# Gathering each page of selected keys and values with four indirect DMAs of 2 KB rows in place of one of 8 KB rows

## The chip, the cores and the metric

The kernel runs on one core of one Trainium2 chip. The metric is the time of one execution on the device, in microseconds, as the median of several runs. The core has TensorE (PE: matrix products, with weight loads shown as PEld), VectorE (DVE), ScalarE (ACT), GpSimd (POOL) and SyncE (SP); DMAs are issued from the queues of SP, ACT and POOL and run on 16 DMA engines that all queues share.

## What is computed

One decoder layer for a prompt of 512 tokens and for 8 samples of 8 new tokens each. A sample has 2048 past tokens in paged pools (16 pages of 128 tokens; a token has 2 heads of 64 floats, 512 bytes). Of the layer, what matters here is the sample's attention over selected blocks:

```python
def gather_past(pool, page_table, new_rows):
    b = page_table.shape[0]
    old = pool[page_table].reshape(b, -1, N_KV_HEADS, HEAD_DIM)
    return jnp.concatenate([old, new_rows], axis=1)
...
ksb = to_blocks(gather_past(cache_k_slc[l], page_table, ks))
vsb = to_blocks(gather_past(cache_v_slc[l], page_table, vs))
...
s = jnp.einsum('bkgqd,bkqmd->bkgqm', qh, k_sel).astype(jnp.float32) * scale
p_slc = masked_softmax(s, (pos_sel <= q_pos[:, None])[:, :, None])
o_slc = jnp.einsum('bkgqm,bkqmd->bkgqd', p_slc.astype(v_sel.dtype), v_sel)
```

The kernel computes the scores against all 2048 past keys of a sample and masks the blocks that are not selected, so it reads every key and value once: 1 MB of keys and 1 MB of values a sample. Beside this there are a compressed branch (from other pools), a window branch (512 tokens from a state), a gated convolution, projections and a feed-forward net.

## The kernel before

All of the program is written by hand, one instruction stream per engine, with semaphores between them. Order in a stream is the order of the code.

Stages, by the profile's time: up to about 125 us the compressed caches of the samples are gathered and compressed; up to about 280 us the input projections and the convolution run; from about 280 to 372 us the samples' attention runs, in four pairs of samples (`gp` 0 to 3), together with products for the adaLN rows (`ada_step`); then the prompt's attention, the output projection and the feed-forward net, which last to the end.

**The ring of pages.** `cring` has `CR` = 4 slots of 2048 columns, 8 KB per partition, 1 MB in all. Loads into it are numbered: 0 to 15 are the compressed caches, and from 16 on, four per pair: pages 16 + 4 gp + b are the selected keys of sample 2 gp + b, pages 18 + 4 gp + b its values (b is 0 or 1). "Page" here is the content of one slot: all 2048 tokens of one sample. Partition p holds 16 consecutive tokens, 8 KB that lie together in the pool. The row numbers for the gather come from `idx`, written once by VectorE (line 1540) from the page table; for the compressed caches from `idq` (line 1537), where a page is already gathered by four indirect DMAs of 2 KB per partition (line 891).

**GpSimd's stream** (from line 905): `key_pages(0)`, `value_pages(0)`, `key_pages(1)`, then for gp = 1, 2: `key_pages(gp + 1)`, `value_pages(gp)`, and at last `value_pages(3)`. `key_pages` waits for the transposes that free its two slots (`keys_turned`), issues two gathers and then the two window loads of 256 KB (`window`, line 883, rows of 2 KB). `value_pages` waits for the last value product of the pair before (bank `("O", gp - 1, 0)`), issues two gathers and two window loads. Behind these come the store of the adaLN rows (line 946) and the scaling of the prompt's probabilities (line 954).

**VectorE's stream.** A page of keys is transposed whole (`turn_page`, line 1829), the window's keys in `turn_window` (line 1838). For gp = 0 the order is: masked scores (line 1910), `turn_window(0)`, compressed scores (1786), window scores, `cmp_probs(1)`, `turn_page(1, 0)`, `turn_page(1, 1)`, `cmp_groups(1)` (lines 1796 and 1797), `turn_window(1)`, then the ranking of blocks (1803 to 1817). For later pairs `turn_page(gp + 1, 0)` stands ahead of the window scores.

**TensorE's stream** (from line 2841): for each pair `values(gp - 1)` (lines 2771 and 2774: x = 0 from the pages of values, x = 1 from the window), compressed and window scores, transposes of probabilities (2439), two `ada_step` (2474), importance and compressed values (2640, 2646), then `scores(gp + 1)` (line 2714), which waits for both page transposes of its pair. `values` waits for the two pages of values.

**SyncE** loads the adaLN weights for the next `ada_step` (line 718, 512 KB each) as their ring is freed.

Of the kernel before, what the change touches and what calls it, by code (L numbers as in the profile page):

```python
# [22 lines left out]
U32 = mybir.dt.uint32  # L23

D = 1024
SEQ, NB, NQ = 512, 8, 8
# [18 lines left out]
CR = 4  # L45
# [8 lines left out]
C_ID, C_P8, C_ROPE, C_ROPEC, C_CAUS, C_CMB, C_CM01, C_NEW, C_WIN, C_OVL, C_TRI, C_ONE, C_END = np.cumsum(  # L54
    [0, 128, 8, 80, 16, 512, 124, 124, 256, 512, 32, 900, 128]).tolist()
# [51 lines left out]
def constants():  # L107

    c = np.zeros((128, C_END), np.float32)
    p = np.arange(128)  # L110
    c[:, C_ID:C_ID + 128] = np.eye(128)
    inv = np.float32(500000.0) ** (-np.arange(8, dtype=np.float32) * np.float32(2.0) / np.float32(16))

    def cs(pos):
        ang = pos.astype(np.float32)[:, None] * inv[None, :]
        return np.concatenate([np.cos(ang), np.sin(ang)], 1)

    for t in range(5):
        c[:, C_ROPE + 16 * t:C_ROPE + 16 * t + 16] = cs(t * 128 + p if t < 4 else PAST + p % NQ)
    c[:, C_ROPEC:C_ROPEC + 16] = cs(p * 16 + 31)  # L120
    c[:, C_CAUS + 384:C_CAUS + 512] = np.where(p[None, :] <= p[:, None], 0, NEG)
    n = np.arange(PNC)
    for t in range(4):
        ok = n[None, :] * 16 + 31 <= (t * 128 + p)[:, None]
        c[:, C_CMB + PNC * t:C_CMB + PNC * (t + 1)] = np.where(ok, 0, NEG)
        c[:, C_CM01 + PNC * t:C_CM01 + PNC * (t + 1)] = ok
    b2, q = p // 64, p % 8
    k = np.arange(TS)
    for gp in range(4):
        ok = (k[None, :] // 8 == (2 * gp + b2)[:, None]) & (k[None, :] % 8 <= q[:, None])  # L130
        c[:, C_NEW + 64 * gp:C_NEW + 64 * gp + 64] = np.where(ok, 0, NEG)
    i = np.arange(512)
    c[:, C_WIN:C_WIN + 512] = np.where((4 * (i % 128) + i // 128)[None, :] > q[:, None], 0, NEG)
    j = np.arange(32)
    c[:, C_OVL:C_OVL + 32] = (p[:, None] * 16 < (j[None, :] + 1) * 64) & (p[:, None] * 16 + 32 > j[None, :] * 64)
    t30 = np.arange(NC1)
    c[:, C_TRI:C_TRI + 900] = np.where(t30[None, :] < t30[:, None], -TIE, 0).reshape(1, 900)
    c[:, C_ONE:C_ONE + 128] = 1
    c[:, C_P8:C_ROPE] = (p % 8)[:, None]
    c[:, C_P8 + 1] = 4 * (p % 8) + p // 32  # L140
    return c


# [112 lines left out]
def decoder_kernel(nc, a, o):  # L256
    at = plan_banks()
    chunks = plan_weights()
    chunk_of = {k: i for i, (k, _) in enumerate(chunks)}

    with ExitStack() as ctx:
        place = {}

        def sb(name, cols, dt=F32, parts=128):
            place[name] = -(-nc.sbuf_base // 32) * 32
            return ctx.enter_context(nc.sbuf_tensor(name, [parts, cols], dt))
# [6 lines left out]
        def sem(name):  # L273
            return ctx.enter_context(nc.semaphore(name))
# [6 lines left out]
        cst = sb("cst", C_END)  # L281
# [13 lines left out]
        cring = arena[:, 0:CR * 2048].rearrange("p (r n) -> p r n", r=CR)  # L295
# [73 lines left out]
        orows = uvT[:, 0:4 * 192]  # L369
        orow = orows[:, :].rearrange("p (g c n) -> p g c n", g=4, c=3)  # L370
        pti = sb("pti", 16, I32, parts=NB)[:, :]
        idx = sb("idx", 8, U32)
        idq = sb("idq", 32, U32)
        pebt = sb("pebt", 2, parts=64)
        pct = sb("pct", 8 * PNC)
# [78 lines left out]
        cache_loaded = [sem(f"cache_loaded{i}") for i in range(CR)]  # L454
# [20 lines left out]
        def ps(key):  # L475
            return bank[at[key][0]]
# [20 lines left out]
        def frees(ins, key):  # L497
            ins.then_inc(bank_free[at[key][0]], 1)
# [16 lines left out]

        def cache(eng, i):

            eng.wait_ge(cache_loaded[slot_of(i)], 64 * (i // CR + 1) if i < 16 else 256 + 16 * (i // CR - 3))
            return cring[:, slot_of(i), :].rearrange("p (s n) -> p s n", s=16)

        def slot_of(i):

            return (i + 2) % CR
# [121 lines left out]
        def early_cols(t):  # L645

            return slice(128 * t, min(128 * t + 128, HALF))
# [22 lines left out]
        def probs(s, k, j):  # L670

            w = 128 * (STEPS[s][0] + 1)
            return psb[(2 * s + k) % 8][:, w * j:w * j + w]

        def column(s, k, j):

            return 8 * (s % 4) + k * len(STEPS[s][2]) + j
# [187 lines left out]
        def _(pool):  # L865
# [31 lines left out]

            def page(i, name, b):

                pool.indirect_dma_start(cring[:, slot_of(i), :], None,  # L900
                                        a[name].rearrange("l n (c s) k d -> (l n c) (s k d)", s=16),
                                        bass.IndirectOffsetOnAxis(idx[:, b:b + 1], 0)
                                        ).then_inc(cache_loaded[slot_of(i)], 16)

            want_emptied(pool, ("chunks",))
            pool.wait_ge(turned, 14)
# [41 lines left out]
            for s in range(NST):  # L948
                t, br, gs = STEPS[s]
                pool.wait_ge(p_recip, s + 1)  # L950
                for k in range(NKV):
                    for j, g in enumerate(gs):
                        c, h, z = column(s, k, j), G * k + g, probs(s, k, j)
# [36 lines left out]
            for t in range(3):  # L990
                pool.wait_ge(h_high, t + 1)
                c = early_cols(t)
# [517 lines left out]
        def _(dve):  # L1510
# [20 lines left out]
            for n in range(4):  # L1531
# [5 lines left out]
            frees(dve.scalar_tensor_tensor(idq[:, :], ps(("pages",))[:, 0:32], 32.0, cst[:, C_P8 + 1:C_P8 + 2].to_broadcast([128, 32]),  # L1537
                                           ALU.mult, ALU.add), ("pages",))
            want_filled(dve, ("chunks",))
            frees(dve.scalar_tensor_tensor(idx[:, :], ps(("chunks",))[:, 0:NB], 8.0, cst[:, C_P8:C_P8 + 1].to_broadcast([128, NB]),  # L1540
                                           ALU.mult, ALU.add), ("chunks",))

            def x_normed(t):
# [520 lines left out]
            for s in range(NST + 1):  # L2064
# [4 lines left out]
                if s < NST:  # L2069
                    t, _, gs = STEPS[s]  # L2070
                    w = 128 * (t + 1)
                    for k in range(NKV):
# [5 lines left out]
                        for j in range(len(gs)):  # L2078
                            c = column(s, k, j)
# [156 lines left out]
            for n in range(2):  # L2236
                cols = slice(512 * n, 512 * n + 512)
                for t in range(6):
# [14 lines left out]
                    if t < 5:  # L2253
                        key, i, P = ("wo", n, t), 5 * n + t, TM[t]
# [890 lines left out]
```

## Time and profile before

| | |
|---|---|
| runs | 904.29, 906.45, 907.99 us; median 906.45 |
| profiled execution | span 917.5 us from the first to the last instruction; the profile gives no other time for it |
| TensorE busy, mean granted clock | 851.0 us (93%), 0.974 |
| VectorE, ScalarE, GpSimd busy | 624.0, 374.3, 307.3 us |
| bytes moved | 138.88 MB, mean 151 GB/s |
| GpSimd's DMA queue (q0) | 9376 packets, 40.31 MB |
| GB/s from 280 to 330 us | 372, 230, 381, 329, 413 for each ten microseconds |

The profile is of one execution, which was longer than the median by 11 us. A row of a timeline gives start, duration, engine, line, operation, output<-input, shape, and in brackets how long the engine was idle before and what released it; "issue" is idle time for which the profile shows no releaser, "remote" a release whose source it does not show. A granted clock of 1.00 is 2.4 GHz, 0.50 is 1.2 GHz.

### The profile page before, as it was taken

To read this page: it belongs to the slowest core of one execution; us is meant where nothing else is said; L and a number is where in the kernel's file an instruction comes from. 1 tells how busy PE (TensorE), PEld (TensorE's weight loads), DVE (VectorE), ACT (ScalarE), POOL (GpSimd) and SP (SyncE) were. 2 spreads that over 40 slices of the span, in tenths; PEclk is the share of its full clock that TensorE was granted. 3 is DMA by queue.
4 is the path that set the end of the run, shared out by engine and by line. 5 is a ranking of instruction groups with operands and counts; after the bars stand their busy time and mean duration, and the time that the engine had idled before them with its cause. 6 is when DMAs were issued, how large, how long until landed. Compare 5 with 4: busy or idle time off the path is not lost.

```text
span 917.5 us, 17109 instructions
## 1 busy us (share of the span) xinstructions
PE 851.0 (93%) x6685; PEld 725.8 (79%) x6685; DVE 624.0 (68%) x1220; ACT 374.3 (41%) x754; POOL 307.3 (33%) x303
## 2 busy tenths in 40 slices
PE   3499999999997789999999998999999999999998
PEld 2366778899994456776777798999999999888886
DVE  2146686388948674668485899988888888434444
ACT  1033262132135434866833664444444446323221
POOL 6456500000003311634400328766677773000000
PEclk9699999999998887999999999999999999999999
DMA  7988922237187987393102554333333324422201
GB/s 207 323 293 320 321 79 75 92 111 262 45 299 259 351 337 275 87 303 108 36 0 92 152 139 123 92 94 92 92 94 93 93 92 165 145 92 93 74 1 52
DMA packets 89167, 138.88 MB, mean 151 GB/s; under 512 B 9268, under 2 KB 59988, under 8 KB 84799
## 3 DMA queue, kind: packets, MB, share of 16 engines
q1 hardware_dynamic: 74866, 96.26, 32.6%
q0 software_dynamic: 9376, 40.31, 12.7%
q10 hardware_dynamic: 4844, 1.21, 0.6%
q8 instruction: 54, 0.88, 0.4%
q14 instruction: 27, 0.21, 0.1%
HBM read 130.58 MB, written 11.31 MB: 155 GB/s over the span
## 4 chain that ended last, share of the span: by engine, by line
PE 74%; DVE 10%; issue 8%; ACT 4%; POOL 2%; another core or an unknown queue 1%; DVEq 0%; POOLq 0%; ACTq 0%
PE bank L2445 17%; PE bank L2447 17%; PE bank L2446 16%; PE bank L2513 4%; PE bank L2439 4%; PE bank L2801 2%; PE bank L2474 2%; PE bank L2714 2%; PE bank L2933 2%; PE bank L2454 2%; PE bank L2455 2%; PE bank L2965 2%; PE bank L2771 1%; DVE ring_lo L535 1%
## 5 line engine op out<-in xcount | busy, mean ns | idle before, releaser
L2445 PE MATMUL bank<-s,ring_hi 128*128 128x288 f32 x620 | 184.1, 297 | 4.5 <-DVE ring_lo L535 4.5
L2446 PE MATMUL bank<-s,ring_lo 128*128 128x288 f32 x620 | 182.9, 295 | 0.0
L2447 PE MATMUL bank<-s,ring_hi 128*128 128x288 f32 x620 | 182.3, 294 | 0.0
L2445 PEld LDWEIGHTS bank<-s,ring_hi 128*128 128x128 f32 x620 | 116.2, 187 | 5.4 <-DVE ring_lo L535 5.3
L2447 PEld LDWEIGHTS bank<-s,ring_hi 128*128 128x128 f32 x620 | 116.8, 188 | 0.0
L2446 PEld LDWEIGHTS bank<-s,ring_lo 128*128 128x128 f32 x620 | 116.4, 188 | 0.0
L535 DVE TENSOR_TENSOR ring_lo<-mem,ring_hi 128x512 fp32r<-128x512 f32 x84 | 106.6, 1304 | 2.1 <-POOL mem L987 1.8
L535 DVE TENSOR_TENSOR dn_w<-wring,dn_w 128x2048 fp32r<-128x2048 f32 (+1 forms) x11 | 23.1, 2097 | 65.8 <-ACT dn_w L532 65.8
L2445 PE MATMUL bank<-dn_w,dn_hi 128*128 128x512 f32 x160 | 62.2, 389 | 0.0
L2446 PE MATMUL bank<-dn_w,dn_lo 128*128 128x512 f32 x160 | 62.2, 389 | 0.0
L2447 PE MATMUL bank<-dn_w,dn_hi 128*128 128x512 f32 x160 | 62.2, 389 | 0.0
L900 POOL DMA_INDIRECT arena<-in_cache_k_slc,idx x8 | 7.9, 991 | 162.0 <-PE bank L2447 152.0
L2445 PE MATMUL bank<-hhi,ws 128*128 128x288 f32 x192 | 56.8, 296 | 0.0
L2447 PE MATMUL bank<-h1hi,ws 128*128 128x288 f32 x192 | 56.6, 295 | 0.0
L2446 PE MATMUL bank<-h1hi,ws 128*128 128x288 f32 x192 | 56.5, 294 | 0.0
L532 ACT CAST dn_w<-wring 128x2048 fp32r<-128x2048 f32 (+1 forms) x11 | 19.3, 1757 | 83.0 <-PE bank L2447 83.0
L535 DVE TENSOR_TENSOR ring_lo<-wring,ring_hi 128x512 fp32r<-128x512 f32 x71 | 52.6, 746 | 0.5 <-ACT ring_hi L532 0.5
L532 ACT CAST ring_hi<-mem 128x512 fp32r<-128x512 f32 x84 | 50.0, 616 | 6.9 <-POOL mem L979 2.3
L979 POOL TENSOR_TENSOR mem<-wring 128x512 f32<-128x512 f32 x20 | 27.1, 1357 | 53.8 <-PE bank L2447 30.1
L532 ACT CAST ws<-wring 128x1024 fp32r<-128x1024 f32 (+2 forms) x18 | 21.8, 1247 | 48.4 <-PE bank L2455 27.2
L891 POOL DMA_INDIRECT arena<-in_cache_k_cmp,idq x32 | 30.6, 955 | 28.0 <-DVE uvT L1605 15.1
L532 ACT CAST ring_hi<-wring 128x512 fp32r<-128x512 f32 x71 | 39.8, 616 | 0.0
(448 smaller groups left out, 2127.4 us busy)
## 6 DMA issues: line engine op xcount, KB each, us to landing
wring<-in_w_gu SPq DMA_DIRECT2D x44, 512.0 KB
wring<-in_w_ada SPq DMA_DIRECT2D x16, 1024.0 KB
wring<-in_w_in SPq DMA_DIRECT2D x10, 1024.0 KB
wring<-in_w_down SPq DMA_DIRECT2D x10, 1024.0 KB
wring<-in_w_ada SPq DMA_DIRECT2D x16, 512.0 KB
proj<-in_x_prompt SPq DMA_DIRECT2D x4, 512.0 KB
mem<-in_state_k_win POOLq DMA_DIRECT2D x8, 256.0 KB
mem<-in_state_v_win POOLq DMA_DIRECT2D x8, 256.0 KB
```

What stands on the lines that cost most here:

```text
L532: return copy(dst, src)
L535: return eng.tensor_tensor(dst, src, hi.bitcast(F32), ALU.subtract)
L891: pool.indirect_dma_start(cring[:, slot_of(i), 512 * n:512 * n + 512], None, a[name].rearrange("l n (c i s) k d -> (l n c i) (s k d)", i=4 ...
L979: ins = pool.tensor_tensor(dst, block_of(f, 0), block_of(f, 1), ALU.subtract)
L2439: return pe.transpose(dst, src, ident[0:P, 0:P])
L2445: pe.matmul(dst, sh, ml, start=first and k == 0, stop=False)
L2446: pe.matmul(dst, sl, mh, start=False, stop=False)
L2447: ins = pe.matmul(dst, sh, mh, start=False, stop=last and k == len(pairs) - 1)
L2454: pe.matmul(dst, s, ml, start=first and k == 0, stop=False)
L2455: ins = pe.matmul(dst, s, mh, start=False, stop=last and k == len(pairs) - 1)
L2474: ins = pe.matmul(ps(key)[32 * j:32 * j + 32, :], cT[:, 32 * kk:32 * kk + 32], w[:, j, :], start=kk == 0, stop=kk == 7)
L2513: ins = pe.matmul(dst, w1v[:, u % 2, j].rearrange("p r h -> p (r h)"), x[:, j // 2, j % 2], start=j == 0, stop=j == 7)
```

## The change

A page of selected keys or values is gathered by four indirect DMAs, each for a quarter of the columns: 2 KB per partition, 4 tokens, 256 KB in all. The same bytes go to the same places. The row numbers are in units of 2 KB, so there are four columns of them per sample, and each page counts 64 on its semaphore instead of 16.

```diff
     c[:, C_P8 + 1] = 4 * (p % 8) + p // 32
+    c[:, C_P8 + 2:C_P8 + 6] = 4 * (p % 8)[:, None] + np.arange(4)[None, :]
     return c
...
-        idx = sb("idx", 8, U32)
+        idx = sb("idx", 32, U32)
...
-            eng.wait_ge(cache_loaded[slot_of(i)], 64 * (i // CR + 1) if i < 16 else 256 + 16 * (i // CR - 3))
+            eng.wait_ge(cache_loaded[slot_of(i)], 64 * (i // CR + 1))
...
             def page(i, name, b):
 
-                pool.indirect_dma_start(cring[:, slot_of(i), :], None,
-                                        a[name].rearrange("l n (c s) k d -> (l n c) (s k d)", s=16),
-                                        bass.IndirectOffsetOnAxis(idx[:, b:b + 1], 0)
-                                        ).then_inc(cache_loaded[slot_of(i)], 16)
+                for n in range(4):
+                    pool.indirect_dma_start(cring[:, slot_of(i), 512 * n:512 * n + 512], None,
+                                            a[name].rearrange("l n (c s) k d -> (l n c) (s k d)", s=4),
+                                            bass.IndirectOffsetOnAxis(idx[:, 8 * n + b:8 * n + b + 1], 0)
+                                            ).then_inc(cache_loaded[slot_of(i)], 16)
...
-            frees(dve.scalar_tensor_tensor(idx[:, :], ps(("chunks",))[:, 0:NB], 8.0, cst[:, C_P8:C_P8 + 1].to_broadcast([128, NB]),
+            frees(dve.scalar_tensor_tensor(idx[:, :].rearrange("p (n b) -> p n b", n=4),
+                                           ps(("chunks",))[:, 0:NB].unsqueeze(1).to_broadcast([128, 4, NB]), 32.0,
+                                           cst[:, C_P8 + 2:C_P8 + 6].unsqueeze(2).to_broadcast([128, 4, NB]),
                                            ALU.mult, ALU.add), ("chunks",))
```

## Rows read from the trace of the kernel before

**Rows 1.** The page: chain of work that ended last, by engine.
```profile
PE 74%; DVE 10%; issue 8%; ACT 4%; POOL 2%; another core or an unknown queue 1%; DVEq 0%; POOLq 0%; ACTq 0%
```
**Rows 2.** The page, groups: line, engine, operation, count | busy, mean ns | idle before.
```profile
L900 POOL DMA_INDIRECT arena<-in_cache_k_slc,idx x8 | 7.9, 991 | 162.0 <-PE bank L2447 152.0
```
**Rows 3.** Timeline of GpSimd: start, duration, line, operation [idle before <-releaser].
```profile
278.83 1.00 POOL L900 DMA_INDIRECT arena<-in_cache_v_slc,idx  x1 [0.30 <-issue]
...
282.58 1.01 POOL L900 DMA_INDIRECT arena<-in_cache_k_slc,idx  x1 [0.30 <-issue]
...
291.53 1.15 POOL L883 DMA_DIRECT2D mem<-in_state_k_win  x2 [6.66 <-DVE arena L1838]
...
309.76 1.00 POOL L900 DMA_INDIRECT arena<-in_cache_v_slc,idx  x1 [8.44 <-PE bank L2774]
...
349.69 1.00 POOL L900 DMA_INDIRECT arena<-in_cache_v_slc,idx  x1 [14.26 <-PE bank L2774]
...
363.14 0.55 POOL L946 DMA_DIRECT2D g_rows<-arows  x1 [9.21 <-DVE arows L1563]
```
**Rows 4.** Timeline of VectorE, 293 to 332 us.
```profile
293.69 2.30 DVE L1829 STREAM_TRANSPOSE mem<-arena 128x2048 f32<-128x2048 f32 x1
295.92 2.27 DVE L1829 STREAM_TRANSPOSE hbuf<-arena 128x2048 f32<-128x2048 f32 x1
298.11 0.33 DVE L1796 TENSOR_REDUCE uvT<-uvT 127x32 f32<-127x128 f32 x1
...
329.72 2.31 DVE L1829 STREAM_TRANSPOSE mem<-arena 128x2048 f32<-128x2048 f32 x1
```
**Rows 5.** Chain in order of time (start, duration, what); last, TensorE's wait total.
```profile
299.65 2.34 PE bank L2714 x62
...
303.25 3.63 issue
...
344.31 1.23 PE bank L2771 x75
345.55 2.09 issue
...
365.33 1.69 PE bank L2771 x109
...
PE bank L2771 <- issue: 7.4, 4, 3.6
```
**Rows 6.** Scores of pair 1 in the chain; windows: length, busy times, clock, DMA share, GB/s.
```profile
283.23 3.70 PE bank L2714 x52
...
283.00:287.00 4.00, 4.00 (x74) 1.18 (x66) 2.41 (x11) 1.70 (x3) 1.57 (x2) 0.55 0.97 397
...
299.60:302.00 2.40, 2.35 (x66) 1.01 (x68) 2.04 (x13) 1.51 (x3) 1.15 (x2) 1.00 0.94 360
```
**Rows 7.** DMA of windows 282:286, 286:288, 299:303, 349:351 and 343:346, in this order.
```profile
DMA packets 212, 1.61 MB, mean 401 GB/s; under 512 B 16, under 2 KB 16, under 8 KB 16
...
DMA packets 208, 0.85 MB, mean 426 GB/s; under 512 B 44, under 2 KB 44, under 8 KB 164
...
q0 software_dynamic: 124, 0.88, 54.9%
q1 hardware_dynamic: 144, 0.54, 39.7%
...
DMA packets 0, 0.00 MB, mean 0 GB/s; under 512 B 0, under 2 KB 0, under 8 KB 0
...
q1 hardware_dynamic: 167, 1.24, 98.4%
```
**Rows 8.** Timelines of GpSimd and VectorE, 3 to 14 us.
```profile
8.16 0.95 POOL L891 DMA_INDIRECT arena<-in_cache_k_cmp,idq  x1 [0.30 <-issue]
...
3.77 0.16 DVE L1540 SCALAR_TENSOR_TENSOR idx<-bank,cst 128x8 uint32<-128x8 f32 x1
13.22 2.31 DVE L1605 STREAM_TRANSPOSE uvT<-arena 128x2048 f32<-128x2048 f32 x1 [9.30 <-DMA arena<-in_cache_k_cmp,idq]
```

## The prediction

> **What bounds the kernel now.** I read the page first. TensorE's work is 74% of the chain that ended last [rows 1], so a change on GpSimd's queue costs only where TensorE comes to wait for it. The gathers that change are 16 instructions, eight for keys and eight for values, of about 0.99 us [rows 2]. The timeline of GpSimd [rows 3] shows where they stand: four per pair of samples (two pages of keys, two of values), each pair of gathers followed by the 2 KB rows of a window load, and each released by a reader of the ring. I number the ring's pages as the code does: 16, 17 keys and 18, 19 values of the first pair; 20, 21 and 22, 23 of the second; and so on to 31. A page of keys is read by a VectorE transpose (line 1829) [rows 4], a page of values by TensorE (line 2771) [rows 5]. Between 294 and 300 us VectorE is the pace: its two transposes run back to back, then the group sums of line 1796, and the scores of the second pair begin 1.5 us behind those, at 299.65 [rows 4, 5]. So what must be asked for every gather is when its last byte lands, and when its reader comes.
>
> **Part 1, the index table.** VectorE writes 32 columns in place of 8, once, near 4 us. It takes 0.16 us now, and VectorE then idles until 13.22 for data [rows 8]. Cost 0: the 9.3 us of waiting hide it; uncovered, four times the columns would be under 0.5 us. The constants' five columns and the counts waited for (64 for every page) add no instruction on the path.
>
> **Part 2, the issue on GpSimd.** 16 gathers become 64. Before, one takes 0.99 us and the 0.30 us idle that stands before each, 1.3 us [rows 2, 3]. The gathers of 2 KB rows of the compressed caches, the very form that is added, take 0.95 and the same 0.30, 1.25 us [rows 8]. So a page takes 4 x 1.25 = 5.0 us of GpSimd instead of 1.3: 3.7 us more each, 59 us over the 16 pages. Most of that lies in idle time: GpSimd waited 152 us before the first, and 9.2 us before the store behind the last [rows 2, 3]. It counts where a reader stands close.
>
> **Part 3, the transfer.** The bytes are the same, 1 MB a page. At 8 KB a row, 1.61 MB went in 4 us (401 GB/s); the window's 2 KB rows went at 426 GB/s [rows 7]. Neither size is faster by itself, cost 0. But four issues bring 256 KB in 1.25 us, 210 GB/s: one stream of such gathers is now held by the issue, where before it was held by the engines. What ends last is the landing of the fourth quarter, counted from its issue. Lower bound: no byte moved in the window from 349 to 351 though a gather was issued at 349.69 [rows 3, 7], so at least 1.3 us, plus 0.6 us for 256 KB at 426 GB/s: 1.9. Upper bound: the fourth quarter of the first compressed page was issued at 8.16, and its reader was released at 13.22: 5.1 us, with SyncE's loads on the same engines [rows 8]. I take 3.7, nearer the upper row: SyncE issues 2 MB of weights at 298, and beside it the gather's queue had 55% and SyncE's 40% [rows 7]. What I leave above the lower row, 1.8 us, is then contention and the confirmation of the write, which no row here parts.
>
> The Trainium skill's page "DMA: Bandwidth & Descriptors" (section "Anatomy of one DMA — SWDGE (gpsimd) path") puts a DMA at about 2.0 us plus bytes over 436 GB/s; an estimate by that page is 2.6 us for a quarter, 1.1 less than I take; the first wait would be 1.1 less and page 27 hidden, and the sum +4.7. The first compressed page landed 8.8 us after its first quarter's issue (8.16 less three steps of 1.25, to 13.22) [rows 8], so the fixed costs overlap; four in a row would be 10.4.
>
> **Part 4, stage by stage.** Pair 1: page 17 is issued by 270 and read at 278, hidden. Pages 18, 19 run from 278.83 to 288.6, the window to 289.7; TensorE reads them at 302, hidden. But pages 20 and 21 stand behind them in GpSimd's order. Their quarters are now issued at 290.0 to 293.75 and 295.0 to 298.8 (before: page 20 at 282.58, page 21 1.3 us later). Page 20 lands near 297.4, page 21 near 298.8 + 3.7 = 302.5. Their transposes began at 293.69 and 295.92 [rows 4], so the second starts 6.6 us late. Behind it on VectorE are queued the group sums, the window's transpose and the ranking; the scores wait for both. TensorE has nothing else in its order: **+6.6 us** (bounds +4.8 and +7.9).
>
> Clock: TensorE now stands for six microseconds before these scores. The scores of the first pair, which followed such waits, took 3.7 us at a granted 0.55; the second pair's took 2.34 us at 1.00 [rows 5, 6]. These are the levels of 1.2 and 2.4 GHz, mixed over a stretch. **+1.2** (0 to 1.4).
>
> Pairs 3 and 4: after the first value product GpSimd has in order 22, 23, window, 28, 29, window, 26, 27. Counted from that product's end (309.46 before, 0.3 ahead of the gather at 309.76), this is 0.3 + 10.0 + 1.2 + 0.3 + 10.0 + 1.2 + 0.3, then the last quarter's issue at 8.8 more, 32.1, and its landing at 35.8. TensorE wants page 27 at 344.31 - 309.46 = 34.9 [rows 5]: **+1.0** (0 to 2.4). Page 28's transpose was at 329.72, 20.3 after the product; it now lands at 0.3 + 10.0 + 1.5 + 3.75 + 3.7 = 19.2: hidden by 1.0 us. Pages 30, 31 follow the product that released the gather at 349.69, land 12.8 us behind it, and are read at 365.33, 16 us behind: hidden. GpSimd is then free 0.3 + 10.0 + 1.2 = 11.5 us behind that product, before 4.2; so of the 9.2 us idle ahead of the store at 363.14 some 2 us are left: hidden. Its next work, the prompt's scaling behind 372, waits for VectorE.
>
> Give-back: in the middle of the first value product TensorE stands 3.63 us with no releaser shown (303.25), with gather and weights together at 95% of the engines just before [rows 5, 7]. The same place in the third pair has 2.09 us (345.55) [rows 5]. With the gather's stream thinned by half and TensorE's stand ahead of it, I take back **-2.0** (0 to -3.6).
>
> Sum: 6.6 + 1.2 + 1.0 - 2.0 = +6.8 us. All of it lies on TensorE's order, and the stages behind 372 us are a chain of dependent work, so I carry it whole. The page gives only the span of the profiled execution, 917.5, 11 us above the median of the runs, 906.45; the sum makes it 924.3, and the median about 913.2.
>
> **The rivals.**
> *A, not slower: the large packets hold up instruction fetch.* TensorE's stands without releaser inside the value products sum to 7.4 us in four [rows 5]. If 8 KB rows in the queue make them, 2 KB rows end them, and with the landing at its lower bound and no loss of clock: 4.8 - 7.4 = -2.6, 903.9. It decides where more comes back than the waits cost, 4.8 us at that bound and 8.8 at my own values. For it: the largest stand falls in a window where gather and weights fill the engines. Against it: from 343 to 346, where the 2.09 us begin, SyncE's queue alone had 98% of the engines and no gather ran [rows 7]. The same skill page (section "Queues, rings and completion order") says that an engine of the DMA switches between queues only at packet boundaries, which would favour this; no row here shows the switch. Chance 0.10; half of it I put beyond 0.5%, for stands at other lines that would go too.
> *B, GpSimd becomes the pace.* Per pair it now needs 4 x 5.0 + 2 x 1.2 + 0.3 = 22.7 us; TensorE's period from the first value product's end to the third's was 39.9 us for two [rows 3, 5]. With the landing at 5.1 us, the first wait is 7.9, page 27's 2.4, page 28's 0.4, the clock 1.4, nothing back: +12.1, 918.6. Chance 0.14.
> *C, hidden.* If quarters issue faster than 1.25 us with the engine's queue hot, or VectorE's other work fills its wait, half of the first wait goes: 6.8 - 3.3 = +3.5, 910.0. For it: nothing but that spans on GpSimd are rough. Chance 0.12.
> *Forecast*: 0.64.
>
> **How the numbers follow.** The likeliest is 913.2. Range 907.5 to 919.0: the lower end is 4.8 + 0 + 0 - 3.6 = +1.2 (907.6), the upper rival B; what is left out is most of A and a loss that repeats in every pair. Measurements of this kernel tell about 0.5%, 4.5 us, from no change. Faster by more: half of A, 0.05. Within: half of A, and C, 0.17. Slower: the forecast and B, 0.78.
>
> **What would show it.** VectorE's second transpose of the second pair about 6 us later against the first scores, idle before it and ended by a DMA; GpSimd's queue four gathers a page at 1.25 us; TensorE's idle before line 2714 at 300 us and a granted clock under 1 there; the stand in the first value product shorter. I am wrong if that transpose is not late (then the landing was never the bound), if the loss is spread over all pairs (B), or if the chain after 372 us takes time back.

## The result and the profile after

The changed kernel takes 922.7 us (median; the kernel before beside it 907.2): a ratio of 1.0194, 95% interval 1.0153 to 1.0234. That is +15.5 us by the medians, where the prediction had +6.8, and outside its range. The profiled execution has a span of 921.7 us at a granted clock of 0.967.

The cost lies in one stage, from GpSimd's first window load to the prompt's first scaling. It can be read off two rows of GpSimd's timeline in each kernel, and cut in three by the value products of TensorE: F, from that window load to the end of the first product (its window's part included); M, on to the end of the third; E, on to the scaling. Two profiles of the kernel before are set beside the one of after, since they differ among themselves: the first is of an execution that was slow for this kernel (a span of 917.5 us), the second, `before_third`, an experiment below, is of one with a span of 905.9. `after_again` is a second profile of the changed kernel.

| us | F | M | E | whole stage |
|---|---|---|---|---|
| before, the profile shown ahead | 33.1 | 39.9 | 21.8 | 94.8 |
| before_third | 31.0 | 37.3 | 21.3 | 89.7 |
| after | 38.6 | 43.3 | 26.5 | 108.4 |
| after_again | 40.2 | 42.2 | 25.8 | 108.2 |
| loss, after against the profile shown ahead | +5.5 | +3.4 | +4.7 | +13.6 |
| loss, after against before_third | +7.6 | +6.0 | +5.2 | +18.8 |
| predicted (6.6 + 1.2 - 2.0; page 27; pages 30, 31) | +5.8 | +1.0 | 0 | +6.8 |

The second loss is the like-for-like one, since both executions, though on two chips, are near their kernel's median: the scaling comes 17.7 us later (375.79 for 358.08), the window load 1.1 us earlier, and behind the scaling about 2 us come back. The first profile had lost 9 to 10 us ahead of its window load (277.37 for 268.42 and 267.37). So the front was near in its sum only against the profile that the prediction was made from, and what lies behind the first value product was too small against both.

The like-for-like loss has two halves. Rows of the whole stage, before_third and after (window, its length, the busy time of TensorE, its weight loads, VectorE, ScalarE and GpSimd, then the granted clock, the share of the DMA engines and GB/s):

```profile
268.42:358.08 89.66, 69.16 (x1581) 46.99 (x1582) 62.35 (x237) 42.13 (x107) 23.68 (x32) 0.87 0.81 313
```

```profile
267.37:375.79 108.42, 78.35 (x1591) 52.95 (x1591) 63.59 (x240) 42.59 (x107) 63.45 (x74) 0.78 0.75 259
```

TensorE is idle for 30.1 us where it was for 20.5, and busy for 78.4 where it was for 69.2, with the same work (ten matmul records are missing from the first row) at a lower granted clock. So about half of the loss is waiting and half is slower matmuls. Against the first profile, itself at 0.84 and 75.6 us busy, nearly all of it is waiting.

The page of after shows where to look: the chain of work that ended last, by engine, and the gathers' group; they answer to [rows 1] and [rows 2].

```profile
PE 71%; POOL 10%; DVE 6%; issue 5%; DMA 5%; ACT 3%; DVEq 0%; POOLq 0%; ACTq 0%
...
L902 POOL DMA_INDIRECT arena<-in_cache_k_slc,idx x32 | 30.6, 957 | 161.6 <-PE bank L2451 151.7
```

GpSimd has gone from 2% to 10% of the chain, and DMA, which was not listed, has 5%. GpSimd's timeline of after answers to [rows 3]; the gather is now line 902, the window 884, the scaling 956.

```profile
280.08 1.01 POOL L902 DMA_INDIRECT arena<-in_cache_k_slc,idx  x1 [0.30 <-issue]
...
288.93 0.94 POOL L902 DMA_INDIRECT arena<-in_cache_k_slc,idx  x1 [0.30 <-issue]
...
348.60 1.00 POOL L902 DMA_INDIRECT arena<-in_cache_v_slc,idx  x1 [9.43 <-PE bank L2778]
...
357.44 0.95 POOL L902 DMA_INDIRECT arena<-in_cache_v_slc,idx  x1 [0.31 <-issue]
360.62 0.55 POOL L948 DMA_DIRECT2D g_rows<-arows  x1 [1.07 <-DVE arows L1567]
375.79 3.45 POOL L956 TENSOR_SCALAR mem<-mem,small,gat 128x128 f32<-128x128 f32 x8 [14.62 <-DVE small L2047]
```

The eight quarters of pages 20 and 21 go out from 280.08 to 288.93, one each 1.25 us; the last starts 21.6 us behind the first window load (267.37). The eight of pages 30 and 31 end the queue at 357.44. The store behind them still finds GpSimd idle for 1.07 us.

VectorE's two transposes of pages 20 and 21 (they answer to [rows 4]), and that of page 28:

```profile
287.59 2.31 DVE L1833 STREAM_TRANSPOSE mem<-arena 128x2048 f32<-128x2048 f32 x1 [3.67 <-DMA arena<-in_cache_k_slc,idx]
294.23 2.31 DVE L1833 STREAM_TRANSPOSE hbuf<-arena 128x2048 f32<-128x2048 f32 x1 [4.33 <-DMA arena<-in_cache_k_slc,idx]
...
329.61 2.31 DVE L1833 STREAM_TRANSPOSE mem<-arena 128x2048 f32<-128x2048 f32 x1 [4.70 <-DMA arena<-in_cache_k_slc,idx]
```

The chain of waits now runs through three landings: page 21, page 27, page 31 (start, us, what). None of the kind stands in [rows 5].

```profile
288.93 5.20 DMA arena<-in_cache_k_slc,idx
...
337.07 6.00 DMA arena<-in_cache_v_slc,idx
...
357.44 10.21 DMA arena<-in_cache_v_slc,idx
```

And TensorE's own timeline: the wait for the second pair's ranking, the first product in two parts with its stand, then the third and the fourth product, each released by a gather.

```profile
297.22 0.61 PE L2644 MATMUL bank<-cst,uvT 127*128 127x32 f32 x2 [6.71 <-DVE uvT L1801]
...
303.82 1.32 PE L2775 MATMUL bank<-arena,hbuf 128*32 128x64 f32 x78 [0.85 <-issue]
...
343.21 1.28 PE L2775 MATMUL bank<-arena,hbuf 128*32 128x64 f32 x75 [1.18 <-DMA arena<-in_cache_v_slc,idx]
...
367.79 3.64 PE L2775 MATMUL bank<-arena,hbuf 128*32 128x64 f32 x128 [4.98 <-DMA arena<-in_cache_v_slc,idx]
```

That fourth product, right behind its wait, runs at the lower level of the clock, 1.2 GHz (granted clock 0.50):

```profile
367.70:371.80 4.10, 4.01 (x138) 3.70 (x138) 0.00 (x0) 0.00 (x0) 0.00 (x0) 0.50 0.07 25
```

What lies beside the late pages is SyncE's next load of the ada weights, 2 MB each time. Beside page 31 it is two DMAs of 1 MB with 8 KB rows, issued at 355.95, in SyncE's timeline; then the engines' share by queue from 358 to 360, right behind the last quarter's issue:

```profile
355.95 1.19 SPq L719 DMA_DIRECT2D wring<-in_w_ada  x2
```

```profile
q1 hardware_dynamic: 81, 0.66, 83.5%
q0 software_dynamic: 22, 0.06, 7.7%
```

The gather's queue (q0) has 7.7% of the engines, SyncE's (q1) 83.5%. The prediction had taken 55 to 40 for the worst, from [rows 7].

### The profile page after: what moved, and what is told of

The parts are those of the page before. It is cut to its first block, busy times and chain, and to the rows that moved or that the text cites. A ratio compares the mean times of both kernels' runs of the same rounds, so it can differ in the third digit from the quotient of the medians.

```text
span 921.7 us, 17157 instructions
## 1 busy us (share of the span) xinstructions
PE 851.5 (92%) x6685; PEld 729.5 (79%) x6685; DVE 624.1 (68%) x1220; ACT 375.1 (41%) x754; POOL 352.4 (38%) x351
## 4 chain that ended last, share of the span: by engine, by line
PE 71%; POOL 10%; DVE 6%; issue 5%; DMA 5%; ACT 3%; DVEq 0%; POOLq 0%; ACTq 0%
PE bank L2449 18%; PE bank L2451 18%; PE bank L2450 18%; POOL arena L902 5%; POOL arena L892 4%; PE bank L2443 3%; PE bank L2517 3%; DMA arena<-in_cache_k_cmp,idq 2%; PE bank L2937 2%; PE bank L2458 2%; PE bank L2459 2%; DMA arena<-in_cache_v_slc,idx 2%; PE bank L2805 2%; PE bank L2969 2%; PE bank L2478 1%
## 5 line engine op out<-in xcount | busy, mean ns | idle before, releaser
L902 POOL DMA_INDIRECT arena<-in_cache_k_slc,idx x32 | 30.6, 957 | 161.6 <-PE bank L2451 151.7
L2517 PE MATMUL bank<-uvT,mem 128*128 128x256 f32 (+1 forms) x160 | 37.0, 389 | 3.7 <-DVE uvT L1609 3.7
```

The costliest lines, as they stand in the source:

```text
L902: pool.indirect_dma_start(cring[:, slot_of(i), 512 * n:512 * n + 512], None, a[name].rearrange("l n (c s) k d -> (l n c) (s k d)", s=4), b ...
L2517: ins = pe.matmul(dst, w1v[:, u % 2, j].rearrange("p r h -> p (r h)"), x[:, j // 2, j % 2], start=j == 0, stop=j == 7)
```

## The experiments

Two theories were on the table at first: P, the pages land late because their small rows share the engines with SyncE's large ones; and I, GpSimd's issue time alone. A third came after the first four runs: S, the stands of TensorE that have no releaser. Each ratio is to the kernel before, beside it on the same chip.

**The kernel before, again.**


> The kernel before once more, for a second profile: its first one had a span of 917.5 us against runs of 904 to 909. I measure the stage of the samples' attention from GpSimd's first window load to its first scaling of the prompt's probabilities: 94.8 us in the first profile, against 108.4 in the changed kernel. Both theories expect 94 to 96 us here, and a span near 905; if the stage itself varies by several microseconds, the comparison of stages is worth little.

917.8 us, span 916.0; the stage is 94.8 us, as in the profile ahead. This chip is a slower one: the kernel before takes 919.6 us on it. That matters for the next three.

**Keys in quarters only, values in quarters only, SyncE's rows smaller.** The first two keep one of the two forms of page, with a table of row numbers for each form (here keys in quarters; `off` picks the table):

```
-                for n in range(4):
...
+                m = 4 if name == "cache_k_slc" else 1
+                w = 2048 // m
+                for n in range(m):
...
+                    pool.indirect_dma_start(cring[:, slot_of(i), w * n:w * n + w], None,
```

> Only the pages of keys are gathered in four 2 KB pieces; values stay at one DMA of 8 KB rows. Then keys 20 and 21 stand behind two quick gathers of values: last quarter issued near 291.4 on the clock of the first profile, landing 5 us later near 296.6, under 1 us late. Both theories (issue; share beside SyncE's loads) expect that the value pages' waits of TensorE (pages 27 and 31, together about 6 us in the changed kernel) are gone and the first wait nearly so: +1 to +3 us against before.

> Only the pages of values are gathered in four 2 KB pieces. Keys 20 and 21 are issued at 290 to 291.3 on the clock of the first profile, as 8 KB rows, and need 5 us of the engines: landing near 297 to 299, 1 to 3 us late. TensorE still waits for pages 27 and 31. Both theories expect +7 to +11 us against before, so most of the loss. If the sum of this and of keys alone is far under the whole (+15.5 us by medians), the two halves need each other: keys are late because values stand in front of them and are quartered too.

The third is the changed kernel with SyncE's ada loads from the second column group on in DMAs of 512 columns, 2 KB a row:

```
+                    if n:
+                        cols = [(c0 + 512 * y, 512) for c0, w in cols for y in range(w // 512)]
```

> The changed kernel, with SyncE's adaLN weights behind the first group loaded in rows of 2 KB (four DMAs of 512 columns) in place of 4 and 8 KB rows; same bytes, same moments, GpSimd untouched. Theory P (share): the 16 DMA engines take turns row by row between SyncE's and GpSimd's queue, so the gather's 2 KB rows get a third beside 4 KB rows and a fifth beside 8 KB rows; with equal rows they get half. Page 31 lands 5 to 7 us behind its last issue instead of 10.2, page 27 about 4.5 instead of 6.0, page 21 about 4.3 instead of 5.2: 5 to 7 us faster than the changed kernel, +9 to +11 against before. Theory I (issue): the landing is set by GpSimd's issue and the completion of its own DMAs: no change, +15.5 against before, page 31 at 10 us.

Measured: 1.0206 (1.0147 to 1.0264), 1.0352 (1.0295 to 1.041) and 1.0531 (1.0473 to 1.0588), so by the medians +19, +33 and +51 us: far above what was expected, the last by 40 us. In the profile of values_quartered the scores of one pair run at 0.2 us a matmul in place of 0.04 (chain in order of time, line 2730):

```profile
287.56 6.37 PE bank L2730 x32
```

No releaser and no landing stands behind this. From 287.5 to 294 the granted clock is 0.50, and GpSimd's queue has 85% of the engines. A clock at half its level explains a factor of two, not of five; whether the gathers beside it do the rest isn't shown. So on this chip something else is added, and the three say nothing on P or I. All three were made again elsewhere (below), where they cost 0, +8 and +12 us.

**The changed kernel, again; SyncE held; halves.** On a chip where the kernel before takes 907.6.

> The changed kernel once more, for its own ratio beside the other variants. The kernel before gave 907 us in the first comparison and 920 in the last one, and keys or values alone cost more there (2.1% and 3.5%) than the whole change did in the first comparison (1.9%). If the loss is that of late landings alone, the whole change costs 15 to 18 us here too, whichever the level of before. If TensorE's stands without a releaser (theory S, new: beside a long stream of gathers TensorE's own stream is held up) differ by chip, the whole costs more than values alone, 35 us or more, where before is at 920.

1.0196 (1.0151 to 1.024), +16.1 us. Page 21 lands 7.6 us behind its last issue here, page 28 8.7, page 31 9.6.

```
             for gp in range(4):
+                cache(sp, (21, 23, 27, 31)[gp])
                 for i in range(done + 6 + 2 * gp, done + 8 + 2 * gp):
                     load(i)
```

> The changed kernel, with SyncE's adaLN loads of each pair held until page 21, 23, 27 or 31 has landed; the same transfers, only later. Theory P (share beside SyncE's rows): page 27 lands 3 to 4 us behind its last issue instead of 6.0, page 31 instead of 10.2, page 21 instead of 5.2: 5 to 8 us faster than the changed kernel of the same call. Theory I (issue): no change. Theory S: no change, or little, since TensorE's stands lie beside GpSimd's own stream.

1.0134 (1.0085 to 1.0182), 6.5 us less than after_again by the medians, though the two intervals overlap. The chain has one landing left:

```profile
283.95 3.79 DMA arena<-in_cache_k_slc,idx
```

3.79 us is what the prediction had taken (3.7) for a page with nothing beside it, and page 21's transpose starts 25.5 us behind the first window load, 7.3 later than in before_held (18.2, below). So page 21 without SyncE's load is 7.3 us late where the sum had 6.6.

The profile doesn't bear out that all of the 6.5 us are the collision's. This execution is 5 us ahead already at the first window load (262.37, for 267.37 and 266.92), long before the first load that is held (287.75). The stage is 103.8 us, 4.5 less than in the changed kernel: F 37.4, M 40.4 and E 26.0. So E is no shorter than in the changed kernel (26.5 and 25.8). TensorE no longer waits for page 31, and stands in its place for 3.78 and 2.80 us with no releaser (chain):

```profile
340.95 3.78 issue
...
358.17 2.80 issue
```

**Halves**: each page by two DMAs of 4 KB rows.

```
+                m = 2 if name == "cache_k_slc" else 2
+                w = 2048 // m
+                for n in range(m):
...
+                    pool.indirect_dma_start(cring[:, slot_of(i), w * n:w * n + w], None,
```

> Each page in two indirect DMAs of 4 KB rows. GpSimd needs 2.5 us a page instead of 5.0 (before: 1.3). Theories P and I: page 21's second half issued near 286 to 287 on the clock of the first profile, landing with the engines' limit near 293: no wait, within 0.3% of before. Theory S: a loss between, about a third of the whole change's.

1.0008 (0.9975 to 1.0041): free. Pages 21 and 31 land late after their last issue, and cost little: VectorE waits 1.63 us for the one, TensorE 0.73 for the other (chain):

```profile
278.70 8.07 DMA arena<-in_cache_k_slc,idx
...
343.97 9.09 DMA arena<-in_cache_v_slc,idx
```

The first of these has no load of SyncE beside it (that comes at 287.00). It is a backlog, by an estimate: two halves bring 1 MB in 2 x 1.25 = 2.5 us, as fast as the engines take it (1 MB at 401 GB/s [rows 7] is 2.6 us), so earlier halves are still under way when the last one is issued. In quarters 1 MB takes 5.0 us to issue, more than it takes to move, and in sync_held the landing follows the last issue by 3.8.

**GpSimd as busy as after, with whole pages.** A first form of this kernel, with 16 bytes per partition, did not fit the on-chip memory and has no time; for it theory I had been put at +4 to +6 us. In the second form, behind every page's one DMA of 8 KB rows, come three indirect DMAs of 8 bytes per partition:

```
+                for n in range(3):
+                    c0 = 2 * (3 * (i - 16) + n)
+                    pool.indirect_dma_start(spill[:, c0:c0 + 2], None, ...
```

> The kernel before with its pages gathered by one DMA of 8 KB rows each, and behind each of them three more indirect DMAs of 8 bytes per partition into memory that nothing reads. GpSimd has as many instructions to issue as in the changed kernel, but no page lands later than in the kernel before by the issue of its own quarters, and its rows are full size. Theory P (the pages land late because their small packets share the engines with SyncE's large ones): only the pages behind the first one of a pair start later, by 3.7 us each, and they land some 3.5 to 4 us after their issue; the late keys page costs a part of the first wait (3 to 5 us), the later pages cost nothing; +3 to +6 us on the kernel before, and no page lands over 6 us after its issue. Theory I (the time of GpSimd's issue alone sets the loss): about as much as the change itself, +13 to +17 us.

1.0099 (1.006 to 1.0138), +7.2 us: between the two theories as they are worded here, and above what theory I had first been put at. What P said of the landings is wrong. A late one is there, with whole pages, of what now ends the burst, the window load (the chain, then VectorE's timeline):

```profile
288.87 8.71 DMA mem<-in_state_k_win
```

```profile
297.67 1.25 DVE L1846 STREAM_TRANSPOSE arena<-mem 128x1024 f32<-128x1024 f32 x1 [5.24 <-DMA mem<-in_state_k_win]
```

SyncE's load was issued at 286.73. And page 28, one DMA of 8 KB rows issued at 314.39, 1.6 us behind the next load (312.75), is turned only 10.5 us later (VectorE's timeline):

```profile
324.92 2.31 DVE L1837 STREAM_TRANSPOSE mem<-arena 128x2048 f32<-128x2048 f32 x1 [4.26 <-DMA arena<-in_cache_k_slc,idx]
```

So it isn't the small rows that lose against SyncE: what GpSimd issues beside that load lands late, whole or not. Pages 30 and 31, issued whole by 347.6 and well ahead of the load at 352.2, cost nothing.

**Keys ahead of values.**

```
             key_pages(0)
+            for b in range(2):
+                pool.wait_ge(keys_turned, b + 1)
+                page(20 + b, "cache_k_slc", 2 + b)
             value_pages(0)
-            key_pages(1)
+            window(1, 0)
```

> The changed kernel with GpSimd's order altered around the first turn: the two keys pages are issued as soon as their buffers come free, ahead of the values pages 22 and 23 and of the window of layer 1, which are needed later. Quarters and SyncE's rows are as in the changed kernel. If the first wait (8.3 us against the kernel before) is a matter of when page 21 is issued, it goes nearly whole: 6 to 9 us less than the changed kernel, +6 to +10 us on the kernel before, with the waits for pages 27 and 31 left as they are. If it is a matter of the share beside SyncE's rows alone, wherever the page stands in the order, the gain is under 3 us, and page 21 still lands over 5 us after its last issue.

1.0154 (1.0112 to 1.0195), +13.6 us: a miss. The transposes of pages 20 and 21 no longer wait, but the window load that was moved behind the values does, and by more (the chain, then VectorE's timeline):

```profile
288.84 10.81 DMA mem<-in_state_k_win
```

```profile
299.75 1.25 DVE L1845 STREAM_TRANSPOSE arena<-mem 128x1024 f32<-128x1024 f32 x1 [12.49 <-DMA mem<-in_state_k_win]
```

The same four pages and a window have to pass GpSimd before the load of SyncE; the order only says which is last.

**Keys alone and values alone, again**, on the chip of the last two (907.5 for the kernel before).

> Keys pages by four DMAs of 2 KB rows, values pages by one of 8 KB rows, once more, beside the other kernels of this call. By the landing of pages: the first wait is shorter than in the changed kernel by the 3.7 us that page 20's neighbour values pages no longer take of GpSimd ahead of it, page 31 is whole again and its 4.7 us are gone; +4 to +9 us on the kernel before. If TensorE's stands without a releaser (theory S) are part of any kernel with mixed rows, +15 us or more, with steps of about 1 us in the scores.

1.0007 (0.9981 to 1.0034), nothing. Page 21's last quarter goes out 14.0 us behind the first window load in place of 21.6 (the values ahead of it take 2.6 us, not 10), and lands 4.6 us later, half a microsecond behind the issue of SyncE's load. The forecast of +4 to +9 was too much.

> Values pages by four DMAs of 2 KB rows, keys pages by one of 8 KB rows, once more. By the landing of pages: keys page 20 and 21 are issued after values pages 18 and 19 and so some 7 us later than in the kernel before, less 2.5 us of their own; pages 27 and 31 are late as in the changed kernel (3 and 4.7 us); +8 to +13 us on the kernel before. If TensorE's stands without a releaser belong to this mix and not to the chip, +25 us or more again, with matmuls of the scores in steps of 0.7 to 1.4 us.

1.0092 (1.006 to 1.0123), +7.6 us. E is 26.3 us, as in after, with the same two rows in the chain and in TensorE's timeline:

```profile
349.40 10.31 DMA arena<-in_cache_v_slc,idx
```

```profile
359.85 3.64 PE L2787 MATMUL bank<-arena,hbuf 128*32 128x64 f32 x128 [5.14 <-DMA arena<-in_cache_v_slc,idx]
```

Keys and values together cost 16, alone 0 and 8: some 8 of it are there only when both are slow. The nearest reason, argued and not tried alone, is that page 21 then stands behind the values' eight quarters and its own.

**Both causes taken away; the hold alone; smaller rows again; the kernel before once more.** All on one chip, 908.3 for the kernel before.

```
             key_pages(0)
-            value_pages(0)
-            key_pages(1)
+            for b in range(2):
+                pool.wait_ge(keys_turned, b + 1)
+                page(20 + b, "cache_k_slc", 2 + b)
+            pool.wait_ge(turned, 16)
+            page(18, "cache_v_slc", 0)
+            window(1, 0)
+            page(19, "cache_v_slc", 1)
+            window(0, 1)
...
+                cache(sp, (19, 23, 27, 31)[gp])
```

> The changed kernel with both suspected causes taken away: GpSimd issues keys pages 20 and 21 ahead of values page 18, then the window of pair 1, then page 19; and SyncE's 2 MB loads of the ada weights wait until the last page issued beside them has landed. If the loss is the issue's order (6.6 us) plus the landing behind SyncE's load (the rest), both waits go: at most +4 us on the kernel before (0 to +4, page 19 being then the late one by 1 to 3 us), 10 us or more below the changed kernel. If a third cost hangs on the 2 KB rows themselves (stands of TensorE, slower transfer), it stays above +6 us on the kernel before.

1.0087 (1.0056 to 1.0117), +6.9 us: 8 less than the changed kernel, yet not the +4 that would have closed the account. F is 29.2 us, better than before's; M is 45.8 and E 27.7, both longer than in the changed kernel. The hold had moved SyncE's load from page 21 onto page 24, whose keys landed late, and the next load fell beside page 28, as it does in the changed kernel (VectorE's timeline, then the chain):

```profile
302.48 2.31 DVE L1840 STREAM_TRANSPOSE mem<-arena 128x2048 f32<-128x2048 f32 x1 [8.65 <-DMA arena<-in_cache_k_slc,idx]
```

```profile
316.67 8.49 DMA arena<-in_cache_k_slc,idx
```

The first collision was moved, not taken away. In E no gather is waited for, and two stands of 4.06 and 3.55 us with no releaser lie in it. A third cost is neither shown nor excluded.

> The kernel before with the same hold on SyncE's loads as sync_held. If the hold is worth something only where pages are issued late, it gives nothing here: the ratio is 1.000 within 0.4%, and the 6.5 us that sync_held gained are the collision's price. If the hold helps any kernel with this order of loads, it is 3 us or more faster than before, and sync_held's gain says nothing on the quarters.

0.9975 (0.9939 to 1.001): nothing that can be told from 1, so the hold by itself makes this kernel no faster. What sync_held gains is then put down to the collision; how much that is stays open: the stage shows 4.5 us, and from the scaling to the end that execution is 2 us longer than that of after (548.0 for 545.9). E is 23.6 us, 2.3 more than in before_third, which may be the hold's own cost or the spread between profiles.

> The changed kernel with SyncE's loads of the ada weights in 2 KB rows, once more, beside the other kernels of this call. If the engines share packet by packet, rows as small as the gather's give the gather half of the engines, page 31 lands 6 to 8 us behind its last issue and not 10, and the time is 3 to 5 us below the changed kernel, +9 to +12 on before. If a page lands behind SyncE's load whatever its rows are, the landing stays near 10 us and the time near +16 us. If the cost seen at first, +49 us, belongs to this form of load and not to the chip, it comes again.

1.013 (1.0073 to 1.0187), +11.8, inside +9 to +12; its interval overlaps that of the changed kernel. The profile says more than the time: E is 23.0 us, against 26.5 and 25.8, and the last product isn't released by a gather any more:

```profile
364.31 1.76 PE L2780 MATMUL bank<-arena,hbuf 128*32 128x64 f32 x109 [0.60 <-DVE small L2089]
```

The last quarter was issued at 357.52, so page 31 landed within 6.8 us. From 358 to 364, in three windows of 2 us, the gather's queue had 36, 12 and 52% of the engines, a mean of 33; in after the same three windows show 8, 29 and 32%, a mean of 23. But the load also went out otherwise: eight DMAs over 4.5 us from 356.86 on, where it had been two over 1.2 us from 355.95 and 356.23. A later and slower issue would also leave more of the engines to the gather, and no run parts the two. Pages 21 and 28 landed 7.9 and 7.8 us behind their issue, against 7.6 and 8.7 in after_again; there SyncE's rows are 4 KB already.

> The kernel before, for its profile on this chip: from GpSimd's first window load to the prompt's first scaling 94.8 us in both profiles so far, and the same again within 1.5 us by every theory, the chip being another.

The stage is 89.7 us, not 94.8 within 1.5: a miss, and a warning that one profile of before leaves 5 us open. Here whole pages land late too, and cost less than a microsecond (the chain, then VectorE's timeline):

```profile
274.95 11.03 DMA arena<-in_cache_k_slc,idx
```

```profile
286.08 2.31 DVE L1829 STREAM_TRANSPOSE hbuf<-arena 128x2048 f32<-128x2048 f32 x1 [0.85 <-DMA arena<-in_cache_k_slc,idx]
```

Four pages, 4 MB, are issued in 6.1 us and need about 10 at 401 GB/s: the transfer is the pace, and has ended before SyncE's load begins at 287.13.

The landings side by side, each from a row of the chain and one of SyncE's timeline:

| page, kernel | last issue | SyncE's load issued | landing after last issue |
|---|---|---|---|
| 21, sync_held | 283.95 | after the page | 3.8 |
| 21, keys_quartered_2 | 279.20 | 4.1 later | 4.6 |
| 21, after | 288.93 | 0.8 later | 5.2 |
| 27, after | 337.07 | 0.9 later | 6.0 |
| 21, after_again | 288.50 | 0.9 before | 7.6 |
| 21, sync_rows_2k_2 | 287.64 | 1.8 before | 7.9 |
| 31, halves_4k | 343.97 | 1.6 later | 9.1 |
| 31, after | 357.44 | 1.5 before | 10.2 |
| window, padded_8k_b | 288.87 | 2.1 before | 8.7 |
| window, keys_first | 288.84 | 2.4 before | 10.8 |

Where the load is out before the last issue, the extra over 3.8 us is 3.8 to 7.0 us; where it comes 0.8 or 0.9 us behind it, 1.4 and 2.2. (Page 31 of halves_4k has its own queue's backlog too.) The 2 MB of SyncE's by themselves are an estimated 5 us at 401 GB/s, so the extra is of the size of that load, but it isn't simply the load's end that the page waits for: in after, page 31 lands at 367.65, 0.8 us before the load's last DMA (368.49), page 21 at 294.13 and that load only at 303.46.

## Why the prediction was wrong

*Index table (part 1), right.* The wider write takes 0.18 us for 0.16 and the first transpose still waits 8.73 us for data.

*Issue (part 2), right.* 1.25 us a quarter; page 21's last quarter starts 21.6 us behind the first window load, where the sum put it at 21.4 (298.8 less 277.37).

*Landing (part 3), the step that failed.* "What ends last is the landing of the fourth quarter", between 1.9 and 5.1 us, 3.7 taken. With no load beside it that is what was measured, 3.79. But the upper bound came from 8.16 us on, in the middle of other loads of SyncE, and it was a bound only for them: beside the ada loads 5.2 to 10.2 us were measured in after (page 28 8.8 at the most). The prediction had seen the load at 298 and the 55 to 40 share [rows 7]; it didn't ask when SyncE issues the next ones (the trace of before has them at 319.84, 340.28 and 358.45) and set each beside the new last issue.

*Page 21, +6.6 with bounds 4.8 to 7.9.* VectorE's transpose is 8.3 us later, 26.9 us behind the window load against 18.6 [rows 3, 4], outside the bounds; 9.2 against before_third; 7.3 with SyncE held. TensorE itself stands 6.71 us for the ranking, where before_third has 1.13. The size is the issue's, plus a microsecond or more of the collision.

*Clock, +1.2: right where it stands, and taken once where it falls more often.* From 297 to 301 us the granted clock is 0.50, its lower level of 1.2 GHz, behind TensorE's stand; it was 1.00 there before [rows 6]. The scores take 3.50 us for 2.34. But it is at 0.50 again from 349.3 to 355, and behind the wait for page 31. E has a mean of 0.75 for 0.94 in before_third, and TensorE is busy in it for 21.5 us for 17.0; in the whole stage for 9.2 us more. No term of the sum had that.

*Give-back, -2.0.* The stand in the first product is 0.85 us for 3.63: 2.8 back. Over the whole stage the stands with no releaser sum to 10.9 us in after, for 12.2 and 13.8 in the two profiles of before: 1.3 to 2.9 back, so the size was right. The reason given for it isn't shown. With the same quarters they sum to 14.9 us in sync_held and to 0.9 in keys_first, where TensorE waits 36 us for others. So they have no fixed size, and what makes them is open.

*Page 27, +1.0.* M is +3.4 to +6.0. Page 27 landed 6.0 us behind its last issue and TensorE waited 1.18, near the term, though the landing was 2.3 us later than taken. Page 28's keys, "hidden by 1.0 us", kept VectorE 4.70 us: their last quarter went out at 320.80 as the sum has it (15.4 us behind the product), and their transpose starts 8.8 us behind that, not 3.7.

*Pages 30 and 31, "hidden".* E is +4.7 to +5.2. Here the margin was 16 - 12.8 = 3.2 us, and a landing of 10.2 in place of 3.7 uses it up and 3.3 more; in TensorE's row the wait is 4.98. This is the longest wait that was taken as none. The margin was also one of the slow execution that the prediction read: in before_third TensorE comes to the fourth product 12.6 us behind the third (336.20 to 348.84), so there even a landing of 3.7 had nothing left. Values in quarters alone show the wait whole (5.14). It is gone in sync_rows_2k_2, with E 23.0, and in sync_held, with E still 26.0; so how much of E's loss is the landing's isn't settled.

*The rivals.* B came nearest, +12.1, with its landing of 5.1 us, and is half right: GpSimd issues from 305.69 to the last quarter of page 27 at 337.07 without a break, and the chain runs through it there, but it idles 9.4 us ahead of page 30. A would have made some kernel with smaller rows faster than the kernel before, and none is. C has nothing for it.

The Trainium skill's page "DMA: Bandwidth & Descriptors", section "Queues, rings and completion order", says that an engine of the DMA changes queues only at packet boundaries. The one comparison that bears on it doesn't contradict it: with SyncE's rows cut from 8 KB to 2 KB, the gather's mean share beside that load went from 23% to 33%, and page 31 came about 3 us sooner, but the load was also issued later and more slowly. No run here shows the switch itself. The same page's section "Anatomy of one DMA — SWDGE (gpsimd) path" gave, as an estimate, 2.6 us for a quarter; the measured 3.8 with nothing beside it, and up to 10.3, decide against it as the figure to cost with.

## What to carry to other kernels

Set a gather's issue time against its transfer time: whole pages (1.3 us to issue, 2.6 to move 1 MB) and halves (2.5) were free, quarters (5.0) made the issuing engine the pace of each burst and let its last piece go out late. Then lay the new last issue over every other queue's large loads, all of them to the end of the stage: a piece issued beside a 2 MB load landed 1 to 7 us later than alone, and a margin of 3 us that looked safe was none. Read such a margin from an execution near the median, and price the clock behind every new wait of TensorE, not behind the first alone. In the three kernels here that reordered or held loads, a collision came up at the next consumer or a stand took the wait's place; none got back to the kernel before.

## What the runs showed of the hardware

One DMA's landing has no fixed value here: 3.8 us from the last issue with no load beside it (sync_held), 8 to 11 behind a backlog of its own queue (halves_4k, before_third), 5 to 11 beside another queue's 2 MB, with rows of 8 KB (padded_8k_b, at most 10.5) as with rows of 2 KB. And the same kernels cost very different amounts on different chips: values in quarters +33 us on the one and +8 on another, with SyncE's small rows +51 and +12, although the kernel before differed by only 12 us between them (919.6 and 907.5). On the first, matmuls of the scores took five times their usual time with no releaser in the trace; its cause stays open.
